# The up projection as seven products for eight in a two-layer encoder trunk, with the down projection behind it

## The reference, cut to what matters

```python
def conv_gated_mlp(x, w_up, conv_w, conv_b, w_down):      # w_up 1024 x 5632, w_down 2816 x 1024
    h = x @ w_up
    hp = jnp.pad(h, ((0, 0), (CONV_W - 1, 0), (0, 0)))    # CONV_W = 3, causal, per column
    hc = conv_b + hp[:, 0:s] * conv_w[0]
    for j in range(1, CONV_W):
        hc = hc + hp[:, j:j + s] * conv_w[j]
    a, g = jnp.split(hc, 2, axis=-1)
    return (jax.nn.silu(g) * a) @ w_down

for i in range(DEPTH):                                     # DEPTH = 2
    ...                                                    # attention; h = h + concat @ w_o[i]
    h = h + conv_gated_mlp(rmsnorm(h, ffn_norm[i]), w_up[i], conv_w[i], conv_b[i], w_down[i])
    gate = jax.nn.sigmoid(rmsnorm(h, ple_norm[i]) @ w_ple_gate[i])
    h = h + (p[i] @ w_ple_proj[i]) * gate
```

## Time and profile before

| | |
|---|---|
| time, median of 3 runs | 2826.71 us (2826.51 to 2827.16) |
| span of the profiled execution | 2822.7 us |
| TensorE busy | 2762.6 us, 14096 matmuls |
| VectorE, ScalarE, GpSimd busy | 1082.2, 980.1, 689.2 us |
| HBM traffic | 126.44 MB, 45 GB/s over the span |

### The profile page before, as it was taken

The page is one execution under the profiler, slowest core; times in us unless marked ns, Lnnn a source line. Parts: engine busy times, 40 slices in busy tenths (PEclk is TensorE's granted clock), DMA queues, the critical chain, the costliest instruction groups (busy, mean ns, idle before and its releaser), DMA issues.

```text
span 2822.7 us, 40008 instructions
## 1 busy us (share of the span) xinstructions
PE 2762.6 (98%) x14096; PEld 2363.0 (84%) x14096; DVE 1082.2 (38%) x1791; ACT 980.1 (35%) x1588; POOL 689.2 (24%) x423
## 2 busy tenths in 40 slices
PE   8999999899999999999999999998999999999999
PEld 8998988788888888887799989877888888888877
DVE  2115672333344433333331156723334433333433
ACT  4336772422222222223343377624222222222232
POOL 3453221122222222221124532111222222222211
PEclk9999999999999999999999999999999999999999
DMA  4110001111111111111111100011111111111112
GB/s 146 50 46 29 21 9 32 43 45 53 45 45 52 45 45 52 45 45 46 34 46 45 48 22 21 9 45 35 47 45 45 52 45 46 50 45 45 52 38 82
DMA packets 133528, 126.44 MB, mean 45 GB/s; under 512 B 5008, under 2 KB 107792, under 8 KB 133424
## 3 DMA queue, kind: packets, MB, share of 16 engines
q1 hardware_dynamic: 132832, 122.65, 14.0%
q0 software_dynamic: 592, 2.46, 0.3%
HBM read 120.85 MB, written 6.60 MB: 45 GB/s over the span
## 4 chain that ended last, share of the span: by engine, by line
PE 96%; DVE 2%; issue 1%; ACT 1%; DMA 0%; POOL 0%; DVEq 0%; SPq 0%; ACTq 0%; POOLq 0%
PE ps L1203 15%; PE ps L1205 15%; PE ps L1204 15%; PE ps L1411 6%; PE ps L1413 6%; PE ps L1409 6%; PE ps L1412 6%; PE ps L1410 6%; PE ps L1414 6%; PE ps L1339 5%; PE ps L1292 3%; PE ps L1320 3%; PE ps L1179 2%; PE ps L1269 2%; DMA h<-in_x 0%
## 5 line engine op out<-in xcount | busy, mean ns | idle before, releaser
L445 POOL TENSOR_TENSOR w_hl<-w_raw,w_hl 128x1024 fp32r<-128x1024 f32 x216 | 519.1, 2403 | 1832.0 <-ACT w_hl L559 1832.0
L559 ACT ACTIVATE w_hl<-w_raw 128x1024 fp32r<-128x1024 f32 x216 | 227.8, 1055 | 770.7 <-PE ps L1205 766.0
L1203 PE MATMUL ps<-w_hl,xT 128*128 128x384 f32 (+1 forms) x1280 | 462.2, 361 | 0.3
L1205 PE MATMUL ps<-w_hl,xT 128*128 128x384 f32 (+1 forms) x1280 | 461.6, 361 | 0.0
L1204 PE MATMUL ps<-w_hl,xT 128*128 128x384 f32 (+1 forms) x1280 | 461.6, 361 | 0.0
L1127 DVE TENSOR_TENSOR h<-ps,h 128x512 f32<-128x512 f32 x352 | 235.5, 688 | 138.9 <-PE ps L1205 138.0
L1414 PE MATMUL ps<-xT,w_hl 128*128 128x512 f32 x704 | 279.0, 396 | 0.0
L1412 PE MATMUL ps<-xT,w_hl 128*128 128x512 f32 x704 | 279.0, 396 | 0.0
L1410 PE MATMUL ps<-xT,w_hl 128*128 128x512 f32 x704 | 279.0, 396 | 0.0
L1409 PE MATMUL ps<-xT,w_hl 128*128 128x512 f32 x704 | 278.7, 396 | 0.0
L1413 PE MATMUL ps<-xT,w_hl 128*128 128x512 f32 x704 | 278.5, 396 | 0.0
(11 more groups left out here) (130 smaller groups left out, 3958.9 us busy)
## 6 DMA issues: line engine op xcount, KB each, us to landing
w_raw<-in_w_up SPq DMA_DIRECT2D x88, 512.0 KB, 3.7
w_raw<-in_w_down SPq DMA_DIRECT2D x44, 512.0 KB, 3.7
w_raw<-in_w_qkv SPq DMA_DIRECT2D x48, 384.0 KB, 3.2
w_raw<-in_w_o SPq DMA_DIRECT2D x16, 512.0 KB, 3.7
w_raw<-in_w_gate SPq DMA_DIRECT2D x16, 512.0 KB, 3.7
bias<-bias_skewed SPq DMA_DIRECT2D x32, 144.0 KB, 2.7
h<-in_x SPq DMA_DIRECT2D x4, 1024.0 KB, 8.7
out<-h SPq DMA_DIRECT2D x8, 512.0 KB, 2.7
```

Of the source, the lines that this page charges most:

```text
L445: nc.gpsimd.tensor_tensor(w_hl[:, slot % 2, 1, :], w_raw[:, slot % 2, :], w_hl[:, slot % 2, 0, :].bitcast(F), ALU.subtract) \
L559: nc.scalar.activation(w_hl[:, slot % 2, 0, :], w_raw[:, slot % 2, :], ACT.Copy) \
L1203: nc.tensor.matmul(dst, lhs[:, k, 0, cols], wh, start=first, stop=False)
L1205: return nc.tensor.matmul(dst, lhs[:, k, 1, cols], wh, start=False, stop=last)
```

## The change

The feed-forward part is now in two stages. First the whole up projection, 22 **units** per layer, each of 256 columns of `w_up` (two blocks of values for even units, two blocks of gates for odd ones) by 1024 tokens. The activations are cut in four quarters A11, A12, A21, A22 (tokens by k), a unit's weights likewise in B11 to B22, and a unit is made of seven products of quarters instead of eight, in the Winograd form of Strassen's scheme:

- Once per layer, `x_raw` (the transposed rows, unsplit) is filled by ScalarE (tokens 0 to 511) and VectorE (512 to 1023). S1 = A21 + A22 comes from VectorE, S2 = S1 − A11, S3 = A11 − A21 and S4 = A12 − S2 from GpSimd, each in two halves of 1024 elements per partition. Of the seven operands (`VARIANTS`) ScalarE makes the high and VectorE the low part, in halves (`variant_high`, `variant_low`), all operands of it in SBUF.
- Per unit, GpSimd makes four sums of weight quarters (512 elements), ScalarE seven high parts (`unit_high`), GpSimd seven low parts, in a ring of seven buffers.
- A product is 4 k-tiles by 3 matmuls of 512 tokens, in one bank. Where two results share a product, its bank is copied (`keep`) and the next product is added on top in the same bank; `combine` on VectorE (C11, C12, C22) adds the copy to another bank and writes `c_up` in SBUF, `copy_c21` on ScalarE writes the last quarter. Three banks per unit, two units in turn. Product 4 of a unit is computed within the next unit.
- The filter's first tap (`tap`, ScalarE) and the other two (`conv`, VectorE) now read `c_up` in SBUF instead of PSUM. The gated rows are stored to HBM (`act_rows`).

Then the down projection of all 11 groups, one behind the other; each group's rows are loaded from HBM (`act_raw`) and split again by ScalarE and VectorE. As the operands need room, `h` is stored to HBM (`h_spill`) before the up stage and loaded again at its end. Weights of the up projection come as 1 MB per unit instead of 512 KB per block. `pT` is loaded and split at the end of the down stage instead of the start of the up stage.

```diff
+FIRST, MIDDLE, LAST = (1, 5, 6, 2, 7, 3), (1, 2, 5, -4, 6, 3, 7), (5, 2, -4, 1, 3, 6, 7, 4)
@@ -1392,27 +1878,39 @@ TensorE
-                def up(slot0, sc, ubase, uc, i, first=False):
...
+                operand = {1: "A11", 2: "A12", 3: "S4", 4: "A22", 5: "S1", 6: "S2", 7: "S3"}
+                def unit(i, c, u):
+                    for n, p in enumerate(products_of(u)):
+                        v, q = (u - 1, 4) if p < 0 else (u, p)
+                        pe.wait_ge(s_u_low, L * PRODUCTS + i * (7 * c) + (products_before(u) + n + 1))
+                        kept_at, combined_at = L * COPIES + i * (4 * c), L * COMBINED + i * (3 * c)
+                        if q == 1 and u >= 2:
+                            pe.wait_ge(s_kept, kept_at + copy_number(u - 1, "before"))
+                        if q == 2 and u >= 2:
+                            pe.wait_ge(s_combined, combined_at + combined_number(u - 2, "C11"))
+                        if q == 5 and u >= 2:
+                            pe.wait_ge(s_combined, combined_at + combined_number(u - 2, "C12"))
+                        if q in (6, 3, 7):
+                            pe.wait_ge(s_kept, kept_at + copy_number(u, {6: "s1", 3: "s5", 7: "s2"}[q]))
+                        if q == 4:
+                            pe.wait_ge(s_combined, combined_at + combined_number(v, "C22"))
+                        xs, at, dst = variant(operand[q]), ring(q), bank_of(v, q)
+                        for k in range(4):
+                            if k % 2 == 0 and (u == 0 or v == 0):
+                                pe.wait_ge(s_variant_low, L * 14 + 2 * VARIANTS.index(operand[q]) + k // 2 + 1)
+                            wh, wl = (at[:, x, k * P:(k + 1) * P] for x in range(2))
+                            nc.tensor.matmul(dst, wh, xs[:, 0, k], start=k == 0 and q in (1, 2, 5), stop=False,
+                                             skip_group_check=True)
+                            nc.tensor.matmul(dst, wh, xs[:, 1, k], start=False, stop=False, skip_group_check=True)
+                            mm = nc.tensor.matmul(dst, wl, xs[:, 0, k], start=False, stop=k == 3, skip_group_check=True)
+                        mm.then_inc(s_u_done, 1)
@@ ScalarE
+                def unit(i, c, u):
+                    unit_high(i, c, u, 3)
+                    tap(i, c, u - 1, 1)
+                    keep_s1(i, c, u)
+                    unit_high(i, c, u, 4)
+                    unit_high(i, c, u, 5)
+                    silu(i, c, u - 1, 1)
+                    keep_s5(i, c, u)
+                    unit_high(i, c, u, 6)
+                    copy_c21(i, c, u - 1)
+                    tap(i, c, u - 1, 0)
+                    unit_high(i, c, u + 1, 0)
+                    keep_s2(i, c, u)
+                    unit_high(i, c, u + 1, 1)
+                    silu(i, c, u - 1, 0)
+                    unit_high(i, c, u + 1, 2)
@@ VectorE
+                sum_s1(0)
+                variant_low("A11", 0)
+                sum_s1(1)
+                variant_low("A11", 1)
+                for name in VARIANTS[1:]:
+                    variant_low(name, 0)
+                    variant_low(name, 1)
...
+                def unit(i, c, u):
+                    conv(i, c, u - 1, 1)
+                    c11(i, c, u)
+                    gate(i, c, u - 1, 1)
+                    conv(i, c, u - 1, 0)
+                    c12(i, c, u)
+                    gate(i, c, u - 1, 0)
+                    c22(i, c, u)
...
+                down_group(0, 0, 0,
+                           {1: lambda: conv(0, 0, last, 1), 4: lambda: gate(0, 0, last, 1),
+                            6: lambda: conv(0, 0, last, 0)},
+                           {0: lambda: gate(0, 0, last, 0), 2: lambda: act_low(0, 0, 1, 0),
+                            4: lambda: act_low(0, 0, 1, 1)})
@@ GpSimd
+                def unit(i, c, u, sums_at):
...
+                    nc.gpsimd.tensor_tensor(weight_of(u, 7), b22, b12, ALU.subtract).then_inc(s_u_sum, 1)
+                    pool.wait_ge(s_u_sum, number + 1)
+                    nc.gpsimd.tensor_tensor(weight_of(u, 5), b12, b11, ALU.subtract).then_inc(s_u_sum, 1)
+                    for n, p in enumerate(order):
+                        if n == sums_at[0]:
+                            t2()
+                        if n == sums_at[1]:
+                            t4()
+                        at = ring(abs(p))
+                        pool.wait_ge(s_u_high, done + (n + 1))
+                        nc.gpsimd.tensor_tensor(at[:, 1, :].rearrange("p (k n) -> p k n", k=4),
+                                                weight_of(u - 1 if p < 0 else u, abs(p)),
+                                                at[:, 0, :].bitcast(F).rearrange("p (k n) -> p k n", k=4),
+                                                ALU.subtract).then_inc(s_u_low, 1)
+                unit(0, 0, 0, (1, 3))
...
+                for half in range(2):
+                    pool.wait_ge(s_variant_sum, L * 2 + half + 1)
+                    variant_sum("S2", half, s1_sum[:, 2 * half:2 * half + 2], quarter("A11", 2 * half))
+                for half in range(2):
+                    variant_sum("S3", half, quarter("A11", 2 * half), quarter("A21", 2 * half))
+                pool.wait_ge(s_h_spilled, L * (16 * TT) + 16 * TT)
+                for half in range(2):
+                    pool.wait_ge(s_variant_sum_p, L * 6 + half + 1)
+                    variant_sum("S4", half, quarter("A12", 2 * half), s2_sum[:, 2 * half:2 * half + 2])
+                unit(0, 0, 1, (2, 4))
@@ SyncE
+                sp.wait_ge(s_u_done, L * PRODUCTS + product_number(UNITS - 1, 5))
+                load_act(0, 0, 0)
+                load_act(0, 0, 1)
+                sp.wait_ge(s_u_done, L * PRODUCTS + product_number(UNITS - 1, 3))
+                for t in range(TT):
+                    sp.dma_start(h[:, t, :], h_spill[t]).then_inc(h_loaded[t // 2], 16)
```

More of the change, by code:

```diff
@@ L528, in _ @@
                             norm_copy(q_nat[:, b], hd * HD, hd).then_inc(s_qn_ready, 1)
[L530 to L538, removed]
+                for j in range(7):
+                    low(O0 + j + 1)
@@ new lines, in _ @@
+                for half in range(2):
[5 more added lines that the diff above has]
+                unit(0, 0, 1, (2, 4))
+                with pool.Fori(0, U_LOOP) as i:
+                    for u in (2, 3):
+                        unit(i, 2, u, (2, 4))
@@ L539, in _ @@
+                unit(0, 0, UNITS - 2, (2, 4))
+                unit(0, 0, UNITS - 1, (0, 3))
+                for slot in range(D0, SLOTS):
                     low(slot)
@@ new lines, in _ @@
+                variant_high("A11", 0)
+                variant_high("A11", 1)
+                for name in ("S1", "S2"):
+                    variant_high(name, 0)
+                    variant_high(name, 1)
+                keep_s1(0, 0, 0)
+                variant_high("A12", 0)
+                variant_high("A12", 1)
+                keep_s5(0, 0, 0)
+                variant_high("S3", 0)
+                variant_high("S3", 1)
+                keep_s2(0, 0, 0)
+                variant_high("S4", 0)
@@ new lines, in _ @@
+                variant_high("S4", 1)
+                unit_high(0, 0, 1, 0)
+                variant_high("A22", 0)
+                unit_high(0, 0, 1, 1)
+                variant_high("A22", 1)
+                unit_high(0, 0, 1, 2)
+                unit(0, 0, 1)
+                with act.Fori(0, U_LOOP) as i:
+                    for u in (2, 3):
+                        unit(i, 2, u)
+                unit(0, 0, UNITS - 2)
+                last = UNITS - 1
+                unit_high(0, 0, last, 3)
@@ new lines, in _ @@
+                keep_s2(0, 0, last)
+                tap(0, 0, last, 1)
+                copy_c21(0, 0, last)
+                act.wait_ge(s_u_done, L * PRODUCTS + PRODUCTS)
+                high(D0 + 1)
+                tap(0, 0, last, 0)
+                silu(0, 0, last, 1)
+                silu(0, 0, last, 0)
+                act_high(0, 0, 1)
+                with act.Fori(0, D_LOOP - 1) as i:
+                    for g in range(2):
+                        high(D0 + 2 * g + 2, 4, i)
+                        high(D0 + 2 * g + 3, 4, i)
+                        act_high(i, 2, g + 2)
```

526 lines of the change are left out of this document (392 added, 134 removed).

## The result

The changed kernel takes **2750.2 us** (median of 4 runs, 2749.6 to 2759.0) against 2826.9 for the kernel before beside it: a ratio of 0.9739, interval 0.9719 to 0.9759 (the quotient of the two medians, 0.9729, lies inside it). Forecast were 2749.5. The time is right to 1 us, but several terms of its sum are not, and they happen to cancel.

A forecast was written before the change was run, and what follows sets the result against it. TensorE, busy for 98% of the span, was taken as the bound, so only fewer matmuls help. −123.2 (saving) + 2·19 (start) + 2·4 (end) = −77.2 us, from 2826.7 to 2749.5 us; range 2712 to 2785.

The forecast's parts named there:

- The saving: Up projection: 264 fewer matmuls per layer at 0.2333 us each, 61.6 us per layer, 123.2 us in all.
- The start: Start of the up stage: unit 0's six products wait for variant sums and low parts, 19 us per layer.
- strict turns of 2.25 + 1.07 us: Start of the up stage: GpSimd sums (2.25) and VectorE two-SBUF instructions (1.07) alternate as one queue, 30.6 us.
- The 1.4 us for the clock: Start of the up stage: added per layer because TensorE's clock falls to 0.50 in gaps.
- rival (a): Start of the up stage: VectorE and GpSimd hardly disturb one another, giving 2715.5 us; chance 12%.
- The upper bound of 23: Start of the up stage: us per layer if the clock's price is twice over.
- The steady unit: Up-projection units after the start: VectorE and GpSimd feed TensorE in time, so the added cost is nothing.
- TensorE needs 84 · 0.2333: Steady up-projection unit: 84 matmuls at the pace traced before the change, 19.6 us.
- The port's 18.8 us per unit: Steady unit: SBUF port shared by VectorE and GpSimd is in use 18.8 of 19.6 us.
- rival (b): Steady unit: the shared port becomes the bound, 20.3 to 20.8 us per unit, 2779 up to 2800; chance 20%.
- The end: End of the up stage: waits around the last products and first down rows, 4 us per layer, between 2 and 8.
- Later groups: nothing: Down-projection groups after the first: 16 additions and two low parts take 13.5 of 22.4 us, so no cost.

The follow-up runs named there:

- e1: Changed kernel with GpSimd's six variant sums per layer replaced by fills, leaving out the real S2, S3 and S4: 2730.3 us, ratio 0.9669.
- e2: Changed kernel with the six variant sums per layer moved from GpSimd to VectorE: 2733.2 us, ratio 0.9679.
- e9: Changed kernel with the ring places of the weights of products 6 and 7 exchanged: 2773.4 us (one run).
- e11: Kernel before the change with 32 unused bytes per partition ahead of `xT`: 2767.7 us, ratio 0.9804.
- e6: Changed kernel with one unused GpSimd subtraction of 240 elements added to each up-projection unit: 2766.6 us, ratio 0.9806.
- e7: Changed kernel with three unused GpSimd subtractions of 240 elements added to each up-projection unit: 2831.9 us, ratio 1.0024.
- e8: Changed kernel with e2, e3 and e4 together, and VectorE's additions for product 4 ahead of its low parts: 2712.0 us, ratio 0.9608.
- e3: Changed kernel with ScalarE's copy of product 6's bank put ahead of its high parts for the first down group: 2745.5 us, ratio 0.9715.
- e4: Changed kernel with the second down group's `w_down` loads put ahead of the last `act_rows` stores on SyncE: 2736.2 us, ratio 0.9683.
- e10: Changed kernel with 32 unused bytes per partition ahead of `x_four`: 2715.3 us, ratio 0.9619.

## Why the prediction was right, and which steps were not

**The saving** (−123.2): as worked out.

**The start** (19 per layer, measured 15.2). The mechanism, strict turns of 2.25 + 1.07 us, is what the timeline shows, and counted from `x_raw` (at 547.2, 1 us sooner than taken) the second halves of S1, S2, A12 and S3 began at 13.6, 20.2, 25.8 and 30.2 us, forecast 13.5, 20.2, 25.8 and 30.2. The six products end at T + 34.4, not T + 36.2. Two sub-terms were too big, by 1.4 and 1.8 us. The 1.4 us for the clock was wrong: the clock was at 0.50 in some of the gaps, but the half products hid it. And from T + 22.4 on I let unit 1's weight sums and low parts take every turn; only three did, as ScalarE's high parts for it stood behind the high parts of S4 and A22. With the 1.0 us of `x_raw`, less 0.4 by which the first matmul came sooner too, that is the 3.8 us between 19 and 15.2. The upper bound of 23 doesn't come out of its own term: with the clock's price twice it is 20.4. e1 and e2 bear out the mechanism against rival (a).

**The steady unit** (nothing): right in that the shared port didn't show, wrong in the pace. It gained 5.5 us per layer, as the step "TensorE needs 84 · 0.2333" took the pace of before as the engine's own. The earlier trace rows show one pace in both places; e9 to e11 show that it hung on the operands' place in memory. The port's 18.8 us per unit was right (18.8 and 19.0 from e6 and e7), and rival (b) was near: e7 has its drawn-out unit with 2.1 us more work. The margin that decided was 0.5 us in 19.3.

**The end** (4 per layer, measured 17.8 and 15.3): the step that failed. The chain through products 6, 7 and 4 and the first down rows was counted right: in e8, where no other instruction stands in front of it, the last 36 matmuls take 12.2 us, 3.8 more than 8.4 and close to the 4 forecast. The sum was wrong in two ways. First, I took ScalarE to be free when product 6 ended; its next instructions were those of the first down group, and they waited for a DMA (986.48). Secondly, I wrote "Later groups: nothing" after adding up engine time alone. I had not followed SyncE's queue, where the loads of group 1 stand behind stores that wait for the last gates. e3 and e4 show one each, and e8 both: those 12.2 us instead of 17.1, and 258.2 instead of 266.7 for the down stage. Each of these gaps also costs half of the clock for about 5 us behind it, which the sum left out here and put in at the start, where it was hidden.

So the errors are −7.6 (start), −11.0 (pace), +25.1 (end), −3.4 (attention, chance): +3.1 us by this table, 2.7 by the spans, and 0.7 in the time, as the median lies 2.0 us above the span and not 4.0. The end lies far outside its own bounds of 2 to 8 us per layer; alone it would have given some 2775 us, inside the whole range of 2712 to 2785, which reaches into rival (b). That three smaller errors took it off again, and so the hit to 1 us, is luck.

## What to carry to other kernels

Where a stage ends, follow every in-order queue, the DMA issues on SyncE included, from the last instruction of the old stage through the first of the new one: what waits there holds whatever is behind it, and at such a seam there is nothing to cover it. Price instructions of VectorE and GpSimd that both read two SBUF tiles as one queue, and give them to the engine with the shorter instruction. And before counting matmuls, look at their pace by operand and at the start addresses of the tiles: they were worth 2% of the kernel before, though its pace was the same in both places looked at.

## What the runs showed of the hardware that I had not expected

- 32 bytes of padding ahead of the large tiles: 0.2333 to 0.2267 us per 512-column matmul, 1.96% of the kernel before's time (e11) and 1.3% of the changed one's (e10). The Trainium skill (TensorE: Matmul & The Clock Gate, Back-to-back issue gap) gives about 216 ns for an isolated matmul of 512 columns and about 131 ns for one in a stream of weight loads and matmuls; the streams here never went below a mean of 226.7, so that the trace does not agree with the 131.
- Two queues of two-input instructions of 1024 elements took strict turns of 3.32 us at the start of the stage, but a VectorE that issues back to back can also hold GpSimd off for more than one instruction: 4.46 us for 1.28 (e1).
- A gap of 4.9 or 5.9 us in TensorE's work is followed by a granted clock of 0.50 for another 5 us; e4 won 8.5 and 6.9 us by removing waits of 5.9 and 5.3. Behind the gaps of 0.8 to 1.5 us in e8 the clock stays at 1.00.
